# Two passages of a two-block transformer kernel: normed outputs added, split and multiplied by the next weights in another order

## The reference

```
def rmsnorm(x, g):
    y = xf * lax.rsqrt(jnp.mean(xf * xf, axis=-1, keepdims=True) + RMS_EPS)
    return (y * g).astype(x.dtype)
def adaln_in(x, g, shift, scale):
    return rmsnorm(x, g) * (1 + scale) + shift
def adaln_out(x, y, g, gate, weight):
    return x + weight * gate * rmsnorm(y, g)
def swiglu(h, w_gu, w_down):
    gu = h @ w_gu
    return (jax.nn.silu(gu[..., :D_FF]) * gu[..., D_FF:]) @ w_down
def ffn_sublayer(x, mod, k, g_pre, g_post, w_gu, w_down):
    h = adaln_in(x, g_pre, mod[k], mod[k + 1])
    return adaln_out(x, swiglu(h, w_gu, w_down), g_post, mod[k + 2], HALF_STEP)
```

## Time and profile before

| | us |
|---|---|
| median of 3 runs | 2894.39 |
| lowest, highest | 2888.77, 2898.87 |
| profiled execution | 2899.97 |
| its span | 2898.2 |
| PE busy in the span | 2813.3 |
| DVE busy | 1802.0 |
| ACT busy | 1399.2 |
| POOL busy | 788.3 |

### The profile page before, as it was taken

One profiled execution on the slowest core, in us unless ns is written; L12 is line 12 of the kernel. 1 busy time (PEld: TensorE's weight loads), 2 busy tenths in 40 slices (PEclk: granted clock), 3 DMA queues, 4 the chain that ended last, 5 costly groups with the idle time before them and its releaser, 6 DMA issues.

```text
span 2898.2 us, 59282 instructions
## 1 busy us (share of the span) xinstructions
PE 2813.3 (97%) x23610; PEld 2694.0 (93%) x23610; DVE 1802.0 (62%) x2418; ACT 1399.2 (48%) x1915; POOL 788.3 (27%) x767
## 2 busy tenths in 40 slices
PE   6999999999999999999998999999989999998999
PEld 4999999999999999999976998999889999987999
DVE  4646747677647567466475555665966566587664
ACT  3434434444435344344444654655754444476542
POOL 1322312114314224033001330321733223055230
PEclk9999999999999999999999999999989999998999
DMA  8765665566666656666611553555325555541554
GB/s 300 255 247 203 233 237 201 198 225 214 233 223 222 224 203 232 218 225 232 219 59 59 166 189 123 189 195 182 112 83 187 192 169 187 191 153 59 175 185 141
DMA packets 151709, 546.40 MB, mean 189 GB/s; under 512 B 16688, under 2 KB 20576, under 8 KB 151136
## 3 DMA queue, kind: packets, MB, share of 16 engines
q1 hardware_dynamic: 147632, 534.84, 54.4%
q10 hardware_dynamic: 3888, 8.86, 0.8%
HBM read 541.80 MB, written 1.84 MB: 188 GB/s over the span
## 4 chain that ended last, share of the span: by engine, by line
PE 91%; DVE 5%; ACT 1%; issue 1%; ACTq 1%; DMA 0%; POOL 0%; SPq 0%; DVEq 0%
PE ps L422 28%; PE ps L423 28%; PE ps L424 27%; PE ps L449 2%; DVE w_lo L402 1%; PE ps L715 1%; PE ps L840 1%; PE ps L824 1%; PE ps L813 1%; DMA modraw<-wmod 0%; ACTq L1592 0%; DVE xT L2001 0%; PE ps L1075 0%; PE ps L1088 0%; PE ps L908 0%
## 5 line engine op out<-in xcount | busy, mean ns | idle before, releaser
L402 DVE TENSOR_TENSOR w_lo<-raw,w_hi 128x1024 fp32r<-128x1024 f32 x874 | 1137.0, 1317 | 674.1 <-ACT w_hi L394 672.4
L422 PE MATMUL ps<-h_hi,w_hi 128*128 128x256 f32 x4928 | 1401.4, 284 | 17.1 <-DVE h_lo L1646 5.0
L423 PE MATMUL ps<-h_lo,w_hi 128*128 128x256 f32 x4928 | 1390.2, 282 | 0.0
L424 PE MATMUL ps<-h_hi,w_lo 128*128 128x256 f32 x4928 | 1386.7, 281 | 0.0
L394 ACT ACTIVATE w_hi<-raw 128x1024 fp32r<-128x1024 f32 x874 | 899.2, 1057 | 527.3 <-PE ps L424 526.1
L422 PEld LDWEIGHTS ps<-h_hi,w_hi 128*128 128x128 f32 x4928 | 930.8, 189 | 37.3 <-issue 18.8
L424 PEld LDWEIGHTS ps<-h_hi,w_lo 128*128 128x128 f32 x4928 | 945.2, 192 | 0.0
L423 PEld LDWEIGHTS ps<-h_lo,w_hi 128*128 128x128 f32 x4928 | 931.1, 189 | 0.8
L2337 POOL CAST u_hi<-ut 128x256 fp32r<-128x256 f32 (+1 forms) x258 | 223.4, 866 | 1380.0 <-DVE ut L1814 786.1
L422 PE MATMUL ps<-u_hi,w_hi 128*128 128x256 f32 (+1 forms) x2064 | 587.1, 284 | 0.0
L423 PE MATMUL ps<-u_lo,w_hi 128*128 128x256 f32 (+1 forms) x2064 | 586.9, 284 | 0.0
(11 more groups left out here) (323 smaller groups left out, 1753.5 us busy)
## 6 DMA issues: line engine op xcount, KB each, us to landing
raw<-wst SPq DMA_DIRECT2D x874, 512.0 KB, 3.4
modraw<-wmod SPq DMA_DIRECT2D x132, 512.0 KB, 5.3
headraw<-wmod SPq DMA_DIRECT2D x12, 512.0 KB, 10.0
mtab<-mixtabs ACTq DMA_DIRECT2D x2, 1673.5 KB, 7.4
xT<-xin ACTq DMA_DIRECT2D x2, 1024.0 KB, 23.5
atab<-attabs ACTq DMA_DIRECT2D x1, 1024.0 KB, 5.6
out<-xT SPq DMA_DIRECT2D x1, 1024.0 KB, 4.8
skew<-sqb ACTq DMA_DIRECT2D x1, 768.0 KB, 3.2
```

The source lines that it names most:

```text
L402: dve.tensor_tensor(w_lo[:, s, :], raw[:, s, :], w_hi[:, s, :], ALU.subtract).then_inc(S("lo_ready"), 1)
L422: pe.matmul(psum, wh, hi, start=start, stop=False)
L423: pe.matmul(psum, wh, lo, start=False, stop=False)
L424: return pe.matmul(psum, wl, hi, start=False, stop=stop)
```

## The change

Both passages get the early form of `pre2`, and every `gu` starts with `first_units`. `pre`, the table `HI`, the plain start of `gu` and its form without late scaling go.

On VectorE `post_dve` now does all eight tiles and, from the fourth step on, also makes the low parts of the stage that follows. GpSimd leaves `post` and gets `pre2`'s additions of squares in both passages instead.

In passage 1 the shift s can no longer be added before the root is known, since h = rstd * (a x) + s. So s is split too and stands as columns 256 and 257 of `h_hi` and `h_lo` (the same number twice), every matmul of this stage is 258 columns wide, and column 256 of a result is the weights times s. VectorE copies it to `shifts`; ScalarE adds it as the bias of Silu, VectorE in the last product.

Buffers `tn` and `hf` go and `sqe` becomes a tile of its own; memory stays as it was otherwise.

```
 def make_plan():
-    post(T, (1, 1))
-    pre(T, (1, 2))
-    gu(T)
+    post(T, (1, 1), shift=True)
+    pre2((1, 2), None)
+    gu(T, shift=True)
     out(T, FC)
     post(T, (1, 2))
...
             if (l, part) == (0, 0):
-                add("pre2", coef=(2, 0), update=None, early=False, early_n=0)
+                pre2((2, 0), None)
...
             def first_units(c, norm):
-                b, h = c["unit"], c["h"] - DC
+                b, h, N = c["unit"], c["h"] - DC, c["N"] + 2 * c["shift"]
                 pe.wait_ge(S("lo_ready"), b + 2)
+                if c["shift"]:
+                    pe.wait_ge(S("shift_ready"), 2)
                 for k in range(DC):
                     pe.wait_ge(S("h_ready"), h + k + 1)
                     for n in range(2):
-                        mm = tile(pe, ..., ps[:, 4 + n, 0:T], h_hi[:, k, 0:T], h_lo[:, k, 0:T], ...)
+                        mm = tile(pe, ..., ps[:, 4 + n, 0:N], h_hi[:, k, 0:N], h_lo[:, k, 0:N], ...)
...
             def gu_pe(c, before):
+                N, b = c["N"] + 2 * c["shift"], c["unit"]
+                first_units(c, before[1])
+                in_unit(pe, b + 2, 0, 1, N)
+                in_unit(pe, b + 3, 0, 3, N)
+                with pe.Fori(1, FC // 2) as i:
...
+            def gate(c, i, j):
+                act.wait_ge(S("gate_scaled"), FC * c["fin"] + 2 * i + (j + 1))
+                if c["shift"]:
+                    act.wait_ge(S("gate_shift"), 2 * i + (j + 1))
+                act.activation(gt[:, j, 0:T], gt[:, j, 0:T], ACT.Silu,
+                               bias=shifts[:, j, 0:1] if c["shift"] else 0.0)
...
             def post_act(c):
                 load_root()
+                if c["shift"]:
+                    act.wait_ge(S("coef_ready"), MODS)
+                    act.activation(h_hi[:, :, T:T + 2], MOD[...].broadcast_to([P, DC, 2]), ACT.Identity)
...
+            def low_part(c, t):
+                dve.wait_ge(S("h_hi_ready"), DC * c["pre2"] + t + 1)
+                dve.scalar_tensor_tensor(h_lo[:, t, 0:T], xT[:, t, 0:T], a, h_hi[:, t, 0:T],
+                                         ALU.mult, ALU.subtract).then_inc(S("h_ready"), 1)
...
+            def gate_part(c, i, j, bank):
+                dve.wait_ge(S("unit_done"), c["unit"] + 2 * j + 1 + 4 * i)
+                if c["shift"]:
+                    dve.tensor_copy(shifts[:, j, 0:1], ps[:, bank, T:T + 1])
+                dve.tensor_tensor(gt[:, j, 0:T], ps[:, bank, 0:T], rstd[:, 0:T], ALU.mult)
+            def up_part(c, i, j, bank):
+                dve.wait_ge(S("unit_done"), c["unit"] + 2 * j + 2 + 4 * i)
+                if c["shift"]:
+                    dve.tensor_copy(shifts[:, j, 1:2], ps[:, bank, T:T + 1])
+                dve.tensor_tensor(sq[:, j, 0:T], ps[:, bank, 0:T], rstd[:, 0:T], ALU.mult)
+                if c["shift"]:
+                    dve.scalar_tensor_tensor(ut[:, j, 0:T], sq[:, j, 0:T], shifts[:, j, 1:2], gt[:, j, 0:T],
+                                             ALU.add, ALU.mult)
...
-            def post_dve(c):
+            def post_dve(c, follower):
+                if c["shift"]:
+                    dve.tensor_tensor(h_lo[:, :, T:T + 2], MOD[...], h_hi[:, :, T:T + 2], ALU.subtract)
                 recip(c, N)
-                mine = DC - POOL_X
-                for t in range(mine + 1):
-                    if t < mine:
+                for t in range(DC + 3):
+                    if t < DC:
                         dve.tensor_tensor(gy[:, t, 0:N], gy[:, t, 0:N], rstd[:, 0:N], ALU.mult)
-                    if t >= 1:
+                    if 1 <= t <= DC:
                         dve.tensor_tensor(xT[:, t - 1, 0:N], xT[:, t - 1, 0:N], gy[:, t - 1, 0:N], ALU.add)
+                    if t >= 3:
+                        low_part(follower, t - 3)
...
-            def post_pool(c):
-                for n in range(POOL_X):
-                    pool.tensor_tensor(gy[:, t, 0:N], gy[:, t, 0:N], rstd[:, 0:N], ALU.mult)
-                    pool.tensor_tensor(xT[:, t, 0:N], xT[:, t, 0:N], gy[:, t, 0:N], ALU.add)
```

More of the change, by code:

```diff
@@ L737, in gu_pe @@
             def gu_pe(c, before):
-                N, b = c["N"], c["unit"]
-                early = before[0] == "pre2" and before[1]["early"]
-                if early:
-                    first_units(c, before[1])
-                    in_unit(pe, b + 2, 0, 1, N)
-                    in_unit(pe, b + 3, 0, 3, N)
-                with pe.Fori(int(early), FC // 2) as i:
+                N, b = c["N"] + 2 * c["shift"], c["unit"]
[3 more added lines that the diff above has]
+                with pe.Fori(1, FC // 2) as i:
                     for j in range(2):
-                        in_unit(pe, b + 2 * j, i, j, N, h=c["h"] - DC if j == 0 and not early else None)
+                        in_unit(pe, b + 2 * j, i, j, N)
                         in_unit(pe, b + 2 * j + 1, i, 2 + j, N)
@@ L1354, in first_qkv_act, with gu_act @@
                 hi_upto(act, d + 14)
[L1356 to L1365 removed]
+            def gu_act(c):
+                b = c["unit"]
+                for j in range(2):
+                    if j:
+                        split_hi(act, b + 5)
+                    gate(c, 0, j)
+                with act.Fori(1, FC // 2) as i:
                     for j in range(2):
                         split_hi(act, b + 2 * j + 2, i)
[L1368 to L1374 removed]
+                        gate(c, i, j)
+                        split_hi(act, b + 2 * j + 3, i)
+            def gate(c, i, j):
[3 more added lines that the diff above has]
+                act.activation(gt[:, j, 0:T], gt[:, j, 0:T], ACT.Silu,
+                               bias=shifts[:, j, 0:1] if c["shift"] else 0.0).then_inc(S("silu_done"), 1)
             def out_act(c):
@@ L1689, in gu_late_dve, with gu_dve @@
+            def gu_dve(c):
+                d = c["unit"]
+                for j in range(2):
+                    gate_part(c, 0, j, (4, 1)[j])
+                    if j:
+                        split_lo(dve, d + 5)
+                    up_part(c, 0, j, (5, 3)[j])
+                with dve.Fori(1, FC // 2) as i:
                     for j in range(2):
                         split_lo(dve, d + 2 * j + 2, i)
-                        dve.wait_ge(S("unit_done"), b + 2 * j + 1 + 4 * i)
-                        dve.tensor_tensor(gt[:, j, 0:T], ps[:, j, 0:T], rstd[:, 0:T], ALU.mult).then_inc(S("gate_scaled"), 1)
+                        gate_part(c, i, j, j)
@@ L1699, in gu_late_dve @@
[L1699 to L1711 removed]
+                        up_part(c, i, j, 2 + j)
```

228 lines of the change are left out of this document (54 added, 174 removed).

## The result

The changed kernel takes 2910.98 us (median of 4 runs, 2909.80 to 2914.01) against 2891.62 us of the kernel before (4 runs, 2888.77 to 2898.87): ratio 1.0062, 95% interval 1.005 to 1.0074. I had forecast 2883.8 us and a range up to 2894. The profiled execution took 2914.01 us, its span is 2912.1.

What follows compares the result with a forecast made beforehand. TensorE, busy 97% of the span, was taken as the bound, with time to win only where it idles or runs at low clock. Gains of 11.9 - 0.97 - 0.3 = 10.6 us gave a 2883.8 us median, range 2876 to 2894.

Steps and rivals of the forecast that it cites:

- The passages: Time from the first VectorE instruction behind the first reciprocal (zero) to the third weight unit: 9.8 and 2.1 us less.
- last low part: VectorE's row in each passage: the eighth low part done 11.3 us behind zero, 2.3 us of it from GpSimd.
- third unit: Third weight unit, where TensorE runs freely: starts 12.9 us behind zero at high clock, 14.4 at low; 13.7 taken.
- GpSimd's hold: GpSimd's additions of squares slow VectorE in each passage: five of six before the last low part, costing 2.3 us.
- 258 columns: First gate stage: 1056 matmuls two columns wider, priced by width at 0.97 us.
- one-column copy: VectorE's 44 copies in the first gate stage: 0.1 us each, hidden beside TensorE's work.
- The stall at the turn: End of the first gate stage, before the down projection's fifth tile: copies make TensorE wait 0.2 to 0.5 us; 0.3 taken.
- The sum for the change alone: Whole kernel: passage gains of 11.9 us less 0.97 for width and 0.3 for the stall, 10.6 us.
- The step that failed: Whole span: the 10.6 us gain taken off the profiled 2899.97 us gives 2889.4, and 2883.8 for the median.
- Rival A: Both passages: GpSimd holds VectorE for its additions' full length, 5.2 us each; gain 4.8 us, 2889.6 us; chance 0.15.
- B: Both passages: TensorE waits at the sixth unit for w_lo, 1.8 us lost each; 2887.4 us; chance 0.13.
- C: First gate stage: 258-wide matmuls leave the path of 256, a slip of 0.015 us each giving 2900 us; chance 0.06.

Runs made afterwards that it cites:

- e1: The changed kernel with its shift columns in unused bytes of stepper, every other buffer at its old place; 2890.84 us, ratio 0.9969 to the kernel before.
- g1: f3 with z, h_hi and h_lo moved 32 bytes further on as well; 2881.61 us, ratio 0.9960 to the kernel before.
- g2: The kernel before, without the change, with f3's unused bytes, so w_hi moved by 32 bytes; 2891.59 us, ratio 0.9998.
- e4: The changed kernel with 96 unused bytes behind w_lo: raw and w_lo at new places, u_hi and u_lo at their old offset within 128 bytes; 2911.90 us, ratio 1.0046.
- e2: The kernel before with only an unused 32-byte buffer added ahead of raw; 2922.74 us, ratio 1.0082.
- g3: e1 with GpSimd's additions of squares 2 columns wide instead of 256; 2872.86 us in one run.
- f1: e1 with 32 unused bytes ahead of raw and 96 behind it; 2903.19 us, ratio 1.0007 to the kernel before.
- f4: e1 with raw and w_lo 64 bytes further on, u at its old offset within 128 bytes; 2891.25 us, ratio 0.9969 to the kernel before.
- i1: e1 with 128 unused bytes between raw and w_lo; 2903.24 us, ratio 1.0033 to the kernel before.
- i2: f3 with 32 more unused bytes ahead of w_lo and 96 behind it; 2897.69 us, ratio 1.0015 to the kernel before.
- f2: e1 with 32 unused bytes ahead of w_lo and 96 behind it, so w_lo alone at the new offset; 2910.54 us, ratio 1.0041 to the kernel before.
- f3: e1 with 32 unused bytes ahead of w_hi and 96 behind it, so w_hi moved by 32 bytes; 2882.25 us, ratio 0.9943 to the kernel before.

## Why the prediction was wrong

The sign was wrong, by a term that the sum did not have. Point by point:

- *The passages.* Forecast gains 9.8 and 2.1 us, read 23.5 - 13.3 = 10.2 and 15.8 - 13.3 = 2.5 from the prediction's starting points, 10.3 and 2.7 by matmul starts. First matmul 3.0 us behind zero, forecast 3.0; last low part 11.6, forecast 11.3; third unit 13.3 in both, forecast 12.9 to 14.4 with 13.7 chosen. That both ends were open holds: e1's passage 1 ended at 14.4 with PE still at 0.70 of the clock from 1592 to 1594.6, the changed kernel's at 13.3 with 1.00 from 1609 on. In the 16 profiles with the change and whole additions, 27 passages end at 13.3 us and 5 at 14.3 to 14.4, none between. Low parts were to come every 1.4 to 1.7 us; the first three come 1.07 apart and the fourth, beside GpSimd's additions, 2.6 (1602.86 to 1605.47).
- *GpSimd's hold.* 3.0 us for 2.3: all six additions fell ahead of the last low part's end instead of five, at 0.5 us each instead of 0.46. The 0.7 us was made up for by other terms, which is luck.
- *258 columns.* 1.3 us for 0.97 in e1's placement, 2.3 ns a matmul or 2.4 us in g1's: the term took the step to depend on the width alone, and it depends on the placement too. The one-column copy takes 0.16 us for the 0.1 taken, inside its bounds, and stays hidden.
- *The stall at the turn.* 0.18 us for 0.3.
- *The sum for the change alone.* 10.6 us forecast; 10.5 (9.3 to 11.8) measured between g1 and g2, where a larger gain in passage 1 and a larger loss in the stage of 258 columns offset each other. e1 against the kernel before gave a ratio of 0.9969 (0.9956 to 0.9982), 5 to 13 us, which holds it as well.
- *The step that failed.* "The profiled execution is 2899.97 us (span 2898.2), so 2889.4": the sum was taken off the whole span, as if every stretch that the diff does not touch kept its time. The description of the change said that memory "stays as it was otherwise", and it does not: the new `shifts` moves every later tile. The weight's low parts came to lie on a multiple of 64 bytes, TensorE's step in the gate stages went from 117.8 to 120.0 ns, and that cost 21 us with the change in place (e1 to e4, on one chip; 20 from e1 to the changed kernel, on different ones) and 24 without it (before to e2). The rivals had places of their own inside the changed code; none had this one.

Rival A had the right engine, but not its size: 5.2 us for the 3.0 that g3 shows, so GpSimd holds VectorE for about half of its time and not for all of it; B did not occur, PE does not wait before the sixth unit; C, the only slower case, has the wrong mechanism: the loss is in the stages of 256 columns too, and lies ahead of the first matmul of 258.

Left open: why the place of the weights matters to TensorE's loads. Every kernel with 120.0 ns in the last gate stage has all three loads of a tile at multiples of 64, but w_hi and w_lo then also lie at like offsets within 512 bytes, and no run moved both off by the same amount; f1, f4 and i1, at 118.3 to 119.0, show that more than the offset within 64 enters, and i2, at 121.2 in one stage and 117.8 in another, that more than the place enters. What is shown is that moving w_lo alone by 32 bytes (e1 to f2) takes the step from 117.8 to 120.0, not which property of the place does it.

## What to carry to other kernels

A new tile is part of the change, however small: compare the first bytes of all tiles before and after, and put it behind the large ones (or into unused bytes) so that nothing moves. When a trace shows a difference ahead of the first changed instruction, look at placement before looking at the change. Where TensorE's own pace bounds the kernel, try the places of the weight tiles as one tries an order: with w_hi moved by 32 bytes the change gave 2882.25 us (0.9943, 0.9923 to 0.9963; g1, with h moved too, 0.9960, 0.9945 to 0.9975), faster than both kernels. The same move gave the kernel before nothing (g2, 0.9998), so a placement is to be measured with the code that it is for, and over all stages: i2 shows that one stage can mislead.

## What was not expected of the hardware

- *The step depends on where the weights lie*, with the same clock, the same instructions and no wait: 117.8 to 120.0 ns by 32 bytes. Which engine writes at the moment does not enter: in the last gate stage of the changed kernel (2745 to 2835 us) the mean step is 120.0 ns whether VectorE, ScalarE, both or none was splitting a weight as the matmul began (208, 135, 111 and 295 matmuls).
- *Down projections run at several steps of their own.* In the view of one tile, the 176 high-part matmuls of the kernel before in the stage behind passage 1:

```profile
L422 PE MATMUL ps<-u_hi,w_hi x176: 284/289/470, 1723.8 to 1791.5; 128*128 x128, 128*128 128x256 f32 x48
```

and two such projections of e1:

```profile
L409 PE MATMUL ps<-u_hi,w_hi x176: 278/279/385, 2271.3 to 2333.3; 128*128 x128, 128*128 128x256 f32 x48
...
L409 PE MATMUL ps<-u_hi,w_hi x176: 278/289/470, 2459.5 to 2527.4; 128*128 x128, 128*128 128x256 f32 x48
```

(1791.5 - 1723.8) / 175 / 3 = 129.0 ns; 118.1 and 129.3 in e1. The last of g2:

```profile
L424 PE MATMUL ps<-u_hi,w_hi x176: 276/283/385, 2821.2 to 2883.4; 128*128 x128, 128*128 128x256 f32 x48
```

118.5 ns, and no projection of g1, g2 or f3 behind passage 1 is slower than 124.0. One profile of each can't tell chance from placement. My guess is that the old placement leaves these stretches to chance, some 6 us for the slowest, and that the wide spread of the kernel before comes from there; no run tested it.
- *A small instruction of GpSimd is not short.* Five additions of 2 columns took 4.45 us in the records (spans there are rough) and the sixth 2.59, about as long as those of 256 or longer, yet VectorE's row came to 8.6 us, with hardly a hold: the prediction's sum without any is 9.0.
